# A two-layer decoder trunk in float32 on one core: another order of attention, gate and router work

## The reference

```python
u = rmsnorm(h, norm_mix_g[l]); cq, ckv, kr, xr, gt = split(u @ w_in[l])
att = mla_mixer(...)     # 8 heads; rmsnorm and rotary on q and k; softmax(q k) v, causal
rnn = rglru_mixer(...)   # width-4 convolution, linear scan, times gelu(gt)
h = h + concat(rmsnorm(att), rmsnorm(rnn)) @ w_out[l]
u = rmsnorm(h, norm_ffn_g[l])
h = h + (swiglu(u) if l == 0 else moe_swiglu(u))   # moe: router logits u @ w_router, top 2 of 8 experts
```

## Time and profile before

| | |
|---|---|
| three runs | 1048.42, 1050.88 (median), 1051.57 us |
| profiled execution | 1043.57 us, its span 1041.8 us |
| busy share of the span | PE 93%, PEld 82%, DVE 70%, ACT 55%, POOL 4% |
| mean granted TensorE clock | 0.941 of full |
| chain that ended last | PE 84%, DVE 9%, ACT 3%, issue 2% |
| DMA | 203.76 MB, mean 196 GB/s |

### The profile page before, as it was taken

How to read it: one execution, slowest core, us unless ns; L and a number is a source line. 1 busy time by engine, 2 the same in 40 slices (tenths; PEclk the granted TensorE clock), 3 DMA queues, 4 the chain that set the end, 5 groups by cost and what they waited for, 6 DMA issues and landing times.

```text
span 1041.8 us, 15698 instructions
## 1 busy us (share of the span) xinstructions
PE 967.9 (93%) x5858; PEld 852.5 (82%) x5858; DVE 730.8 (70%) x967; ACT 572.9 (55%) x769; POOL 40.6 (4%) x67
## 2 busy tenths in 40 slices
PE   5999967999999999999948989999999999999995
PEld 3864735899999999874726989898989898989893
DVE  5564664656666554565663559897989798989893
ACT  4465161544545443455151457767776877686771
POOL 4140010000000000001000000000000000000000
PEclk9998865999999999999866989999999999999998
DMA  8503011345558573504030419998999899989971
GB/s 262 166 23 116 26 42 40 104 141 182 181 162 225 155 210 93 166 1 142 21 121 1 142 40 351 339 338 314 347 350 328 323 335 362 329 315 340 360 289 43
DMA packets 120018, 203.76 MB, mean 196 GB/s; under 512 B 5874, under 2 KB 73740, under 8 KB 119964
## 3 DMA queue, kind: packets, MB, share of 16 engines
q1 hardware_dynamic: 119504, 202.81, 56.8%
q10 hardware_dynamic: 460, 0.23, 0.1%
HBM read 201.98 MB, written 1.05 MB: 195 GB/s over the span
## 4 chain that ended last, share of the span: by engine, by line
PE 84%; DVE 9%; ACT 3%; issue 2%; DMA 0%; ACTq 0%; POOL 0%; DVEq 0%; POOLq 0%
PE ps L2151 20%; PE ps L585 11%; PE ps L2176 11%; PE ps L587 11%; PE ps L586 11%; PE ps L1747 3%; DVE wlo L1207 3%; PE ps L1822 2%; PE ps L2109 2%; ACT whi L843 1%; PE ps L1853 1%; PE ps L1945 1%; PE ps L1752 1%; PE ps L1870 1%; PE ps L1941 1%
## 5 line engine op out<-in xcount | busy, mean ns | idle before, releaser
L1207 DVE TENSOR_TENSOR wlo<-raw,whi 128x1536 fp32r<-128x1536 f32 (+4 forms) x296 | 437.0, 1504 | 90.3 <-ACT whi L843 88.2
L843 ACT ACTIVATE whi<-raw 128x1536 fp32r<-128x1536 f32 (+4 forms) x296 | 376.3, 1284 | 163.6 <-PE ps L587 83.6
L585 PE MATMUL ps<-uhi,whi 128*128 128x272 f32 (+1 forms) x576 | 171.3, 297 | 2.9 <-DVE ulo L1225 2.9
L587 PE MATMUL ps<-uhi,wlo 128*128 128x272 f32 (+1 forms) x576 | 169.1, 293 | 0.0
L586 PE MATMUL ps<-ulo,whi 128*128 128x272 f32 (+1 forms) x576 | 168.9, 293 | 0.0
L2151 PE MATMUL ps<-whi,xeh 128*128 128x320 f32 (+1 forms) x512 | 124.8, 325 | 0.0
L2151 PE MATMUL ps<-whi,xel 128*128 128x320 f32 (+1 forms) x512 | 123.6, 323 | 0.0
L2151 PE MATMUL ps<-wlo,xeh 128*128 128x320 f32 (+1 forms) x512 | 123.5, 323 | 0.0
L585 PEld LDWEIGHTS ps<-uhi,whi 128*128 128x128 f32 (+1 forms) x576 | 111.3, 193 | 9.3 <-issue 8.7
L586 PEld LDWEIGHTS ps<-ulo,whi 128*128 128x128 f32 (+1 forms) x576 | 111.8, 194 | 0.0
L587 PEld LDWEIGHTS ps<-uhi,wlo 128*128 128x128 f32 (+1 forms) x576 | 111.4, 193 | 0.0
(11 more groups left out here) (285 smaller groups left out, 1374.9 us busy)
## 6 DMA issues: line engine op xcount, KB each, us to landing
raw<-in_moe_w_down_dram SPq DMA_DIRECT2D x24, 1536.0 KB, 7.4
raw<-in_moe_w_gate_dram SPq DMA_DIRECT2D x16, 1536.0 KB, 8.0
raw<-in_moe_w_up_dram SPq DMA_DIRECT2D x16, 1536.0 KB, 8.2
raw<-in_moe_w_gate_dram SPq DMA_DIRECT2D x16, 1280.0 KB, 7.1
raw<-in_moe_w_up_dram SPq DMA_DIRECT2D x16, 1280.0 KB, 6.4
raw<-in_ffn_w_gate_dram SPq DMA_DIRECT2D x11, 1024.0 KB, 5.3
raw<-in_ffn_w_up_dram SPq DMA_DIRECT2D x11, 1024.0 KB, 5.3
raw<-in_ffn_w_down_dram SPq DMA_DIRECT2D x8, 1408.0 KB, 7.0
```

Source lines behind the costliest of these rows:

```text
L585: pe.matmul(dst, wh, xh, start=start, stop=False, skip_group_check=True)
L587: return pe.matmul(dst, wl, xh, start=False, stop=stop, skip_group_check=True)
L843: act.activation(placed(whi, s, src), src, ACT.Copy).then_inc(hi_done, 1)
L1207: dve.tensor_tensor(placed(wlo, s, src), src, placed(whi, s, src).bitcast(F32), ALU.subtract).then_inc(lo_done, 1)
```

## The change

- Layer by layer, the scores of tiles 0 and 1 are moved ahead of gate blocks 1 to 3 on TensorE. Tile 1's scores now lie in `u32`, tile 2's overlap `uhi` and stay behind the gate blocks.
- The gelu is done chunk by chunk, four times 272 columns, in between the other work; a first small exp on ScalarE comes right after the query scales.
- The meta values of tile 0 are split in two ("meta" and "values"); the values of tile 1 follow scores 2 at once, those of tile 2 follow the rnn sum of squares; outputs of the tiles are turned later. In layer 0, `out_turned(2)` stands ahead of the fourth half block; in layer 1 there are three half blocks instead of four.
- The first norm of a layer and the rnn norm are summed to all 128 partitions at once (`total`); the two spreads "n1bc" and "rnbc" go, and the reciprocals run on 128 partitions.
- Router: for each chunk c, behind the next `wo` block, TensorE makes one transposed logits matmul and two transposes of u (`chosen`). POOL sums the squares of chunks 1 to 6 into one. The top two are found on logits that aren't normed; the gates are worked out later, in the first expert. The low parts of expert pieces 1 and 2, and ScalarE's high parts of them, come after the token parts. The transposes of hT go into the first expert.
- The first pair of experts is written out; expert 0 has no `result`, `combine` or `add_expert`. The loop has two turns.

The diff, cut to its core:

```diff
-ATTENTION = [[("scores", 0), ("scores", 1), ("values", 0), ("scores", 2), ("out", 0), ("values", 1), ("rnss", None),
-              ("out", 1), ("rnbc", None), ("values", 2), ("out", 2)],
-             [("scores", 1), ("scores", 2), ("values", 1), ("rnss", None), ("out", 1), ("rnbc", None), ("values", 2),
-              ("out", 2)]]
+ATTENTION = [[("scores", 0), ("scores", 1), ("gt", 1), ("meta", 0), ("gt", 2), ("values", 0), ("gt", 3), ("scores", 2),
+              ("values", 1), ("out", 0), ("rnss", None), ("values", 2), ("out", 1), ("out", 2)],
+             [("scores", 1), ("gt", 1), ("gt", 2), ("gt", 3), ("scores", 2), ("values", 1), ("rnss", None),
+              ("values", 2), ("out", 1), ("out", 2)]]
+GT_BANK = (5, 7, 4, 7)
...
             if what == "scores":
                 for h in range(NH):
                     add("s", t, h)
+            elif what == "gt":
+                add("gt", t, bank=GT_BANK[t])
+            elif what == "meta":
+                add("p", t, META, bank=6)
             elif what == "values":
-                for h in items(t):
-                    add("p", t, h, bank=6 + h % 2)
-                add("o", t, bank=5)
+                if t:
+                    for h in items(t):
+                        add("p", t, h, bank=6 + h % 2)
+                add("o", t, bank=5 - t % 2)
             elif what == "out":
-                add("ot", t, bank=4)
+                add("ot", t, bank=4 if t else None)
             else:
-                add(what, bank=4)
+                add(what)
         for m in range(KD):
-            add("wo", m)
+            add("wo", m, bank=None if l == 0 else m % 3)
+            if l and m == 4:
+                pl.add(("ut", 0, 0), 4)
+                pl.add(("ut", 1, 0), 6)
...
+            pl.add("lgT", 3)
+            pl.add(("ut", 0, 1), 5)
+            pl.add(("ut", 1, 1), 7)
+            add("n2ss", bank=2)
+            pl.add("lg", 3)
+            pl.add("cum", 3)
+            for t in range(2):
+                for hf in range(2):
+                    pl.add(("ht", t, hf), 4 + 2 * t + hf)
...
-        scores = [u32, score1, score2]
+        scores = [u32, u32[:, :, NMETA:], score2]
...
+                    metas(0)
+                metas(1)
+                if l == 0:
+                    average_power(0)
+                metas(2)
+                average_power(1)
+                average_power(2)
...
+                    for m in range(1, KD - 1):
+                        pool.wait_ge(nsq_done, 3 * KD + m + 1)
+                        pool.tensor_tensor(qT[:, 0, NMETA:T], qT[:, 0, NMETA:T], qT[:, m, NMETA:T], ALU.add)\
+                            .then_inc(nsum_done, 1)
+                        pool.wait_ge(nsum_done, m)
...
+            def root_all(b, dst, n, done):
+
+                act.wait_ge(filled, b.ready())
+                act.activation(dst, bank(b), ACT.Sqrt, bias=eps[:, :], scale=1.0 / n).then_inc(emptied[b.bank], 1)
+                act.wait_ge(emptied[b.bank], b.before + 1)
+                mark().then_inc(done, 1)
...
+                mark(ACT.Exp)
...
+                mix(l, N_IN)
+                act.wait_ge(b_done, l + 1)
+                gate_square(0)
+                if l == 0:
+                    exponentials(0)
+                exponentials(1)
+                gate_square(1)
+                gate_tanh(0)
+                mix(l, N_IN + 1)
+                gate_square(2)
+                gate_tanh(1)
+                mix(l, N_IN + 2)
+                gate_square(3)
+                gate_tanh(2)
+                for c in range(CH - 1):
+                    rnn_square(c)
+                exponentials(2, between)
+                rnn_square(3)
+                mix(l, N_IN + 3)
+                if l == 0:
+                    out_high(0)
+                root_all(B[l, "rnss"], rr[:, :], DH2, rn_root)
                 for h in range(1, NH, 2):
-                    turned(t, h)
+                    turned(2, h)
                     if h == 3:
                         rn_high()
+                out_high(1)
...
+            w(0, 0, 0)
+            for hf in range(2):
+                for t in range(2):
+                    act.wait_ge(filled, B["ut", t, hf].ready())
                     act.wait_ge(rstd_done, POWERS[1, "n2"])
                     act.activation(uhi[:, :, :].rearrange("p k t -> p (k t)")[:, t * D + hf * 512:t * D + hf * 512 + 512],
-                                   ps[:, b.bank, :], ACT.Copy, scale=rv[:, t + 3:t + 4]).then_inc(tok_hi, 1)
-            for t in range(2):
-                for hf in range(2):
-                    take(B["ht", t, hf], acc[:, t, hf * 512:hf * 512 + 512], cols=slice(0, 512))
+                                   ps[:, B["ut", t, hf].bank, :], ACT.Copy, scale=rv[:, t + 3:t + 4]).then_inc(tok_hi, 1)
+            w(0, 0, 1, 2)
...
+                if l == 0:
+                    maxima(0)
+                maxima(1)
+                gelu_inner(0)
+                mix(l, N_IN)
+                gelu_gate(1)
+                gelu_times(0)
                 if l == 0:
                     turned(0, META)
+                gelu_inner(1)
+                gelu_gate(2)
+                gelu_times(1)
+                gelu_inner(2)
+                gelu_gate(3)
+                gelu_times(2)
+                maxima(2)
+                gelu_inner(3)
+                turned(1, 0)
+                if l == 0:
                     averages(0)
-                    gelu_times()
-                    maxima(2)
+                turned(1, 2)
+                gelu_times(3)
+                turned(1, 4)
+                if l == 0:
                     normed(0)
-                for h in range(0, NH, 2):
-                    turned(1, h)
-                    if l and h == 2:
-                        gelu_times()
-                    mix(l, N_IN + h // 2)
+                turned(1, 6)
+                mix(l, N_IN + 1)
                 turned(1, META)
+                averages(1)
                 if l == 0:
                     out_low(0)
-                averages(1)
-                rows(l, "rnn", 1)
+                mix(l, N_IN + 2)
+                turned(2, 0)
+                dve.wait_ge(rn_root, l + 1)
+                dve.reciprocal(rr[:, :], rr[:, :]).then_inc(rn_done, 1)
+                turned(2, 2)
+                rn_scaled((0, 1))
                 normed(1)
+                turned(2, 4)
+                rn_scaled((2, 3))
+                turned(2, 6)
+                rn_low()
+                turned(2, META)
+                mix(l, N_IN + 3)
+                averages(2)
                 out_low(1)
...
+                def chosen(c):
+
+                    b = B["lgT"]
+                    if c == 0:
                         fill(pe, b)
-                        pe.wait_ge(rows_done, ROWS_DONE[l, "rnn"])
-                        spread(b.bank, 0, 1).then_inc(filled, 1)
-
-                halves = range(4)
+                        pe.wait_ge(rw_in, 16)
+                    pe.wait_ge(u_done, c + 1)
+                    q = pe.matmul(ps[0:NE, b.bank, 0:SEQ], rw[:, c, :], u32[:, c, NMETA:T], start=(c == 0), stop=(c == KD - 1))
+                    if c == KD - 1:
+                        q.then_inc(filled, 1)
+                    for t in range(2):
+                        b = B["ut", t, c // 4]
+                        lead, n = TILES[t + 1]
+                        if c % 4 == 0:
+                            fill(pe, b)
+                        q = pe.transpose(ps[:, b.bank, c % 4 * P:c % 4 * P + P], u32[:, c, lead:lead + n], ident)
+                        if c % 4 == 3:
+                            q.then_inc(filled, 1)
...
+                    if m == 2:
+                        out_turned(2)
...
+                    if l and m:
+                        chosen(m - 1)
...
+                    chosen(KD - 1)
+                    b = B[l, "n2ss"]
+                    pe.wait_ge(nsum_done, KD - 2)
                     pe.wait_ge(nsq_done, 4 * KD)
                     for t in range(2):
                         lead, n = TILES[t + 1]
-                        for k in range(KD):
-                            q = pe.matmul(ps[:, b.bank, t:t + 1], qT[:, k, lead:lead + n], one[:, :], start=(k == 0),
-                                          stop=(k == KD - 1))
+                        for c in (0, KD - 1):
+                            q = pe.matmul(ps[:, b.bank, t:t + 1], qT[:, c, lead:lead + n], one[:, :], start=(c == 0),
+                                          stop=(c == KD - 1))
+                    q.then_inc(filled, 1)
+                    b = B["lg"]
+                    fill(pe, b)
+                    pe.wait_ge(lgs_done, 1)
+                    for t in range(2):
+                        q = pe.transpose(ps[:, b.bank, t * NE:(t + 1) * NE], rr[0:NE, t * P:(t + 1) * P], ident[0:NE, 0:NE])
...
+                    if first and not p:
+                        hidden_state(0)
+                        hidden_state(1)
```

(15 more changed lines are left out.)

396 lines of the change are left out of this document (181 added, 215 removed).

## The result

The changed kernel takes 1001.47 us (median of 4 runs, 999.05 to 1002.53) against 1051.22 for the kernel before (4 runs, 1048.42 to 1052.71): 0.9526 of the time, 95% interval 0.950 to 0.9553. I had forecast 1015.4 us, from 1003 to 1028.

A forecast was written before the change was run, and what follows sets the result against it. Bound by chains of short steps at low clock in both attentions and the router. 0.9 + 16.7 + 12.7 - 1.4 - 4.6 + 14.0 = 38.3, less 2.8: 35.5 us; 1043.57 becomes 1008.1, plus 7.3 gives 1015.4 us, range 1003 to 1028.

The forecast's parts named there:

- What bounds the kernel: Both attention stages and the router, 148 us: no engine full, chains of short steps handing over, low clock lengthening TensorE's part.
- First norms: Start of each layer: the dropped spread saves 0.5 us of full TensorE per layer, 0.9 together.
- Attention up to the sum of squares: Both layers, last kT operation to rnn sum of squares: ends 36 us after it in layer 0, 32.5 in layer 1.
- The third rival of the list: Both attentions: gelu chain leads, holding maxima 2 and copies in VectorE's order; half of 29.4 us lost, 1030; chance 0.1.
- The same work with the reciprocal in between I put at 11.6: Layer 0 attention, values of tile 2: 11.6 us, ending at 164.6, 15.9 us earlier than before.
- a rival at 1003 us: Clock stays up: first gate blocks, rnn sums and part of the values faster, some 12 us more gained; chance 0.12.
- the cold case: Gate blocks 2 and 3 of both layers take 5.5 us instead of 3.1: 9.6 us lost, 1025; chance 0.2.
- Hand-overs: Some twenty on the new path at 0.14 us each, left out of the step times: 2.8 us added.
- Riders: Seven behind w_out blocks, one logits matmul and two transposes each: 0.66 us apiece, 4.6 us, all on the path.
- GpSimd: POOL's six added squares of 256 columns, 1.3 us each: bounds 0 to 1.3 us at the end, taken as nothing.
- Router: From end of last w_out block to first expert: 13.9 us instead of 27.9, gain 14.0; gather 6.2 us.
- Experts: Loop unchanged, pairs still 103.1 us; first expert from -1 to +2, taken as 0. Longer pairs would show it wrong.
- The median of the runs is 7.3 above the profiled execution: Last step of the sum: 7.3 us added to the profiled 1008.1 to give the forecast median 1015.4 us.

The follow-up runs named there:

- e5: Changed kernel with gate blocks 1 to 3 ahead of the scores again in both layers: 1010.35 us, 9.0 more.
- e8: Kernel before with sixteen dummy matmuls a layer in TensorE's pauses between rnn sum of squares and values of tile 2: 1042.16 us, 0.9956 of the kernel before.
- e17: Changed kernel with TensorE waiting before the values of tile 2 until VectorE has taken the reciprocal and scaled all four chunks: 1017.57 us, 16.3 more.
- e6: Changed kernel with TensorE also waiting for ScalarE's root of the rnn sum before the values of tile 2, both layers: 1002.22 us.
- e13: Kernel before with the rnn sum of squares written to 128 rows instead of one: 1045.89 us, 0.9978 of the kernel before.
- e14: Changed kernel with the turn of tile 1 back between the rnn sum of squares and the values of tile 2: 1001.27 us.
- e7: Changed kernel with all riders (logits matmuls and transposes) behind the last output block: 1001.25 us.
- e3: Changed kernel with the small tensor pick placed behind all expert tensors: 996.86 us, 4.4 less than the unedited changed kernel on the same chip.
- e4: Kernel before with the unused tensor pick added where the change puts it, moving the experts' tensors by 128 bytes: 1047.96 us, one execution.
- e18: Kernel before, unedited, profiled once more: 1053.72 us, span 1051.9, mean clock 0.93.
- e10: e3 plus twelve small fp32 dummy matmuls a layer in the values of tile 1: 993.97 us, 0.9493 of the kernel before.
- e9: e3 plus one-pass dummy matmuls in the kT stage, behind each spread and each of the first scores: 1016.0 us, 19 more than e3.

## Why the prediction was wrong, point by point

**What bounds the kernel.** Right: the gain came from the three chains of short steps that I named, and the view that showed it (busy time far under the window, a low clock) was the right one.

**First norms.** Forecast 0.9 and found 0.6 for the whole of these stages, but that closeness is luck. From the norm's sum of squares to the next group of sums it is 22.8 us before and 21.7 after in both layers, so each norm gives 1.1, and not 0.5, as if a part of the copy and of the waits, which I took as covered, had lain on the path too. What hides it is the clock elsewhere, in layer 1 above all: the twelve records of the key stage that took 5.42 us at 1.00 take 7.11 at 0.76.

**Attention up to the sum of squares.** Right within 1.5 us. Counted from the last kT operation, gate block 3 is scaled after 16.4 us (forecast 16.5), maxima 2 are done after 22.2 (22.7), the sum of squares ends after 34.8 in layer 0 (36.0) and 31.0 in layer 1 (32.5). The overlap of maxima and gate blocks is what e5 takes away again (9.0 us). The third rival of the list, gelu in the lead, did not come: VectorE waits 0.87 us for each tanh and catches up.

**The first step that failed: "The same work with the reciprocal in between I put at 11.6".** I took the duration of tile 2's values from the earlier trace rows, at 0.50, as if the low clock belonged to these values. It belonged to the pauses ahead of them. The change takes both pauses away, and the values run at 1.00: 9.2 us a layer. The attentions gave 9.3 us more than forecast: 4.9 are the values, 2.7 the earlier ends of the sums (1.2 and 1.5), and 1.7 the stretches behind, which no run takes apart (the end in layer 0 was also summed wrongly, 0.6 - 1.6 is -1.0 and not -0.8). e8 shows that the clock makes the difference, e17 that a long pause makes the clock, and e6, e13, e14 and e5 show that a short pause, the form of the sum, the row of values and the order of the scores do not. I had this case as a rival at 1003 us with a chance of 0.12, and spoke against it with the row that showed TensorE full at 0.50. It came true only in part, for the first gate blocks and the sums still ran partly at half clock (the sums 3.1 to 3.2 us, the clock 0.6); that its number lies so near is luck, since half of the miss is elsewhere. And that row shows only that full work does not bring the clock back at once, not what keeps it when it is up. The Trainium skill, "TensorE: Matmul & The Clock Gate", "HAM oscillation — how this bites in real kernels", says that gaps between bursts let the gate fall. I read it as speaking for the cold case, though this change removes the gaps: by that rule, rightly applied, the warm case was the likelier. e17 agrees with it: 0.51 in the values behind a pause of 4.47 us.

**Hand-overs.** 2.8 us added for twenty of them; the durations that I had taken from the trace held them already, and no stage shows them on top. Too much by 2.8.

**Riders.** 0.66 each forecast; found 0.89: VectorE's additions behind two blocks in a row are 3.74 us apart with a rider (551.25 to 554.99) and 2.85 in the kernel before (587.09 to 589.94). Seven cost some 6.2, not 4.6, and e7 agrees that it is on the path, for nothing is gained or lost by moving them. The rest of the +8.3 is block 3 (1.4, as forecast) and a start at a clock of 0.50, from 533.2 to 536.2, behind the pause of 2.49 us (some 1.3). These three come to 8.9, so one of them is a little too high.

**GpSimd.** Nothing at the end, as taken. The trace of after does show the two together; the first add stands beside a low part, the fourth has VectorE idle:

```profile
539.42 1.53 POOL L822 TENSOR_TENSOR qT<-qT 128x256 f32<-128x256 f32 x1 [11.56 <-ACT qT L893]
541.59 1.41 POOL L822 TENSOR_TENSOR qT<-qT 128x256 f32<-128x256 f32 x1 [0.63 <-ACT qT L893]
...
548.58 0.74 POOL L822 TENSOR_TENSOR qT<-qT 128x256 f32<-128x256 f32 x1 [1.83 <-ACT qT L893]
```

An add takes 0.74 us alone and 1.4 to 1.5 beside VectorE's low parts, which stay at 1.22. The Trainium skill, "SBUF — State Buffer", "SBUF: two separate sides", has the two exclude each other, the one that starts first keeping the way for its whole length; the trace agrees, for in all three slow adds VectorE had started first, and it shows no cost for VectorE. The last add, which counts, meets an idle VectorE.

**Router.** Forecast 13.9, found 13.7: the step by step count holds within 0.4 us at each step up to the gather, which took 5.6 and not 6.2.

**Experts.** "The loop itself is unchanged" was true of the instructions and not of the addresses: +3.6 us, of which e3 and e4 show 2.6 to 4.0. The prediction had named longer pairs as a sign that it was wrong, and they are longer, though not for VectorE's pace. The first expert alone is within 0.3 us.

**The second step that failed: "The median of the runs is 7.3 above the profiled execution".** This is half of the miss, 7.7 of 14 us. I carried a difference as a constant without knowing where it lies. e18 shows most of it in stretches at low clock. 3.7 of its 10.1 us are in the router, whose 64 records of sums and logits the change mostly removes or moves to the riders; 3.1 are in the key stage, where the profile of the changed kernel already holds 1.7 of them (7.11 us between 5.42 and 8.13). The executions of the changed kernel lie between 999 and 1003 us, its profiled one among them. That these two are all of the reason is argued and not shown; why one execution of the kernel before keeps its clock and another doesn't stays open.

## What to carry to other kernels

A duration at half clock is not a property of the instructions: before carrying it over, look at the pauses of TensorE ahead of it, and ask whether the change removes them; a few useless matmuls in a pause are a cheap test (e8, e10) and can also cost 19 us (e9). A new small tensor ahead of large ones moves their addresses: put it last. And a distance between a profiled execution and the median has a place in the trace; find it before adding it to another kernel.

## What the runs showed of the hardware

- TensorE at 5.00 busy of each 5 us can stay at 0.50: for 20 us in e9, with thin matmuls of 16 rows and dummies between them. Busy time alone does not tell the clock; e10 has 1.00 at 4.3 of 5.
- A clock of 1.00 stays for a while when TensorE goes idle, and then falls: in e17 TensorE is idle from 151.6 to 156.06, and the clock is 1.00 until 153.6, 0.69 in the next us and 0.50 from 154.6. What is issued behind the pause starts at half clock.
- Moving the expert tensors by 128 bytes in each partition makes the 384-column matmuls 1.7% slower (4.24 against 4.17 us for 24) and leaves the 320-column groups alike. Why wasn't tried.
- The kernel before runs anywhere from 1043 to 1055 us, with a mean clock of 0.941 at the short end and 0.927 to 0.93 at the long one; the two profiles do the same work and differ mostly by where the clock falls (e18).
